# Thirteen weight loads sent as partitions 0 to 125 and 126 to 127

## What is computed

```
q = (x @ w_q).reshape(B, S, 8, 2, 128)
s = einsum('bshcd,cnd->bshcn', q, sub_keys)      # 8 heads, two sets of 128 keys
sv, si = top_k(s, 16)                            # best 16 of each set
best_s, pos = top_k(sums of all 16 x 16 pairs, 16)
gate = softmax(best_s)
hid = gelu(einsum('td,ted->te', xt, u[e]))       # 128 experts for each token
y   = einsum('te,ted->td', gate * hid, v[e])
```

## Time and profile before

| | |
|---|---|
| median of three runs | 1507.61 us |
| the profiled execution | 1510.85 us |
| its span, first to last instruction | 1508.9 us |
| TensorE, VectorE, ScalarE, GpSimd busy | 1340.3, 1015.8, 705.3, 492.7 us |
| moved by DMA | 597.94 MB, mean 396 GB/s |
| of it by gathers (q0) | 536.90 MB |
| of it by plain loads and stores (q1) | 60.01 MB |

### The profile page before, as it was taken

The page is one execution under the profiler, slowest core; times in us unless marked ns, Lnnn a source line. Parts: engine busy times, 40 slices in busy tenths (PEclk is TensorE's granted clock), DMA queues, the critical chain, the costliest instruction groups (busy, mean ns, idle before and its releaser), DMA issues.

```text
span 1508.9 us, 16214 instructions
## 1 busy us (share of the span) xinstructions
PE 1340.3 (89%) x5068; PEld 729.8 (48%) x5068; DVE 1015.8 (67%) x2399; ACT 705.3 (47%) x2128; POOL 492.7 (33%) x527
## 2 busy tenths in 40 slices
PE   9999998987898888889989899999989998888886
PEld 8877554433353454444447645444335443334322
DVE  1137877777757777686654587777787767666655
ACT  2223554545544545436554244654554544444443
POOL 0003333334333333333320233343333433333331
PEclk9999999999999999999999999999999999999999
DMA  9749999999999999999989699999999999999996
GB/s 370 252 168 412 384 419 420 420 421 422 421 421 421 421 421 421 421 420 405 421 348 410 238 405 420 421 421 422 421 422 421 416 422 421 422 421 420 412 423 265
DMA packets 92393, 597.94 MB, mean 396 GB/s; under 512 B 10386, under 2 KB 13074, under 8 KB 26004
## 3 DMA queue, kind: packets, MB, share of 16 engines
q0 software_dynamic: 73728, 536.90, 86.0%
q1 hardware_dynamic: 18580, 60.01, 10.5%
HBM read 595.82 MB, written 1.05 MB: 396 GB/s over the span
## 4 chain that ended last, share of the span: by engine, by line
PE 41%; DMA 29%; DVE 16%; ACT 9%; issue 3%; POOL 0%; SPq 0%; ACTq 0%; DVEq 0%; POOLq 0%
DMA uv<-in_peer_uv_dram,expert 28%; PE y L694 24%; DVE uv L1780 7%; PE spare L581 3%; PE y L540 3%; PE px L383 2%; ACT diag L1331 2%; PE y L408 2%; ACT L1323 2%; ACT wts L1325 1%; DVE key_idx L1628 1%; DVE hit L1620 1%; ACT act_hid L1323 1%; DVE key_idx L1622 1%; DVE key_top L1625 1%
## 5 line engine op out<-in xcount | busy, mean ns | idle before, releaser
L694 PE MATMUL y<-uv,diag 128*128 128x512 f32 x1868 | 911.7, 624 | 147.1 <-ACT diag L1331 146.2
L1780 DVE CUSTOM_DVE_ANT_0 uv<-px,uv 128x1024 f32<-128x1024 f32 x512 | 619.1, 1220 | 343.5 <-DMA uv<-in_peer_uv_dram,expert 334.3
L1158 POOL DMA_INDIRECT uv<-in_peer_uv_dram,expert x512 | 487.2, 952 | 961.4 <-PE y L694 752.5
L694 PEld LDWEIGHTS y<-uv,diag 128*128 128x128 f32 x1868 | 338.1, 195 | 581.8 <-issue 295.6
L1323 ACT ACTIVATE act_hid<-hid 128x1 f32<-128x1 f32 x512 | 102.8, 201 | 567.2 <-DVE hid L1780 563.1
L1331 ACT ACTIVATE diag<-ident,wts 128x128 f32<-128x128 f32 x468 | 187.9, 402 | 44.2 <-ACT wts L1325 1.5
L1325 ACT ACTIVATE wts<-act_hid,gate 128x1 f32<-128x1 f32 x512 | 150.7, 294 | 16.6
L1323 ACT ACT_TABLE_LOAD x47 | 60.3, 1283 | 0.8
L1791 DVE SCALAR_TENSOR_TENSOR vsum<-uv,wts,vsum 128x1024 f32<-128x1024 f32 x41 | 52.5, 1281 | 8.3 <-ACT wts L1325 8.0
L1780 DVE DVE_READ_ACCUMULATOR2_ANT hid<- 128x1 f32 x512 | 42.3, 83 | 0.0
L1497 DVE TENSOR_TENSOR probs<-spare,bias 128x320 f32<-128x320 f32 x16 | 7.6, 473 | 45.9 <-PE spare L436 45.9
(11 more groups left out here) (309 smaller groups left out, 1290.9 us busy)
## 6 DMA issues: line engine op xcount, KB each, us to landing
uv<-in_peer_uv_dram,expert POOLq DMA_INDIRECT x512, 13.6
uv<-in_na_w_dram SPq DMA_DIRECT2D x9, 512.0 KB, 8.9
w_q<-in_peer_w_q_dram SPq DMA_DIRECT2D x8, 512.0 KB, 11.8
uv<-in_mla_w_out_dram SPq DMA_DIRECT2D x8, 512.0 KB, 6.7
bias<-in_na_bias_dram SPq DMA_DIRECT2D x16, 160.0 KB, 7.0
w_vu<-in_na_w_dram SPq DMA_DIRECT2D x4, 512.0 KB, 9.0
w_latq<-in_na_w_out_dram SPq DMA_DIRECT2D x4, 512.0 KB, 6.7
latkv_room<-in_peer_w_q_dram SPq DMA_DIRECT2D x4, 512.0 KB, 11.0
```

Source lines behind the costliest of these rows:

```text
L694: last = T.matmul(Y[t][:, c, :], diag[:, acc_no(n) % DIAGS, :], uv[:, n % RING, 1, c * 512:(c + 1) * 512], start=False, stop=half_done)
L1158: pool.indirect_dma_start(uv[:, n % RING, :, :].rearrange("p h d -> p (h d)"), None, uv_table, bass.IndirectOffsetOnAxis(ap=expert[:, g % ...
L1780: V_.tensor_tensor_reduce(out=rows, in0=px[:, :, :], in1=rows, scale=1.0, scalar=0.0, op0=ALU.mult, op1=ALU.add, accum_out=hid[:, k:k + 1] ...
```

## The change

Thirteen loads of layer 0 are issued as two DMAs each, one for partitions 0 to 125 and one for 126 and 127. Source, target and order stay as they were. Each part adds 16 to the same semaphore, so the waits for them rise.

```
+LATE_KEPT = [4, 6, 7]
+SPLIT = 126
...
-                pe.wait_ge(s_kept[g % PH], 32 * (layer + 1))
+                pe.wait_ge(s_kept[g % PH], 32 * (layer + 1 + (g % PH in LATE_KEPT)))
...
-                    pe.wait_ge(s_latkv, 16)
+                    pe.wait_ge(s_latkv, 32)
...
-                    pe.wait_ge(s_latq, 16)
+                    pe.wait_ge(s_latq, 32)
...
-                pe.wait_ge(s_kn, 16)
+                pe.wait_ge(s_kn, 32)
...
-                pe.wait_ge(s_vu, 16)
+                pe.wait_ge(s_vu, 32)
...
-                    pe.wait_ge(s_qn, 16)
+                    pe.wait_ge(s_qn, 32)
...
-                    pe.wait_ge(s_qrs, 32)
+                    pe.wait_ge(s_qrs, 64)
...
+            def load_in_two(dst, src, done):
+                for part in (slice(0, SPLIT), slice(SPLIT, P)):
+                    sp.dma_start(dst[part], src[part]).then_inc(done, 16)
+
             def kept_load(layer, h):
                 for c in range(2):
+                    if layer == 0 and h in LATE_KEPT:
+                        load_in_two(kept[h][c], peer_w_q[layer, h, c], s_kept[h])
+                        continue
                     sp.dma_start(kept[h][c], peer_w_q[layer, h, c]).then_inc(s_kept[h], 16)
...
                         for dst, piece, done in loads[h]:
-                            sp.dma_start(dst, piece).then_inc(done, 16)
+                            load_in_two(dst, piece, done)
```

More of the change, by code:

```diff
@@ L1053, in layer_loads @@
                         sp.wait_ge(s_full[rest_bank(LATE[j])], job["rest", LATE[j]])
-                        kept_load(0, (4, 6, 7)[j])
+                        kept_load(0, LATE_KEPT[j])
                 if layer:
```

## The result

The changed kernel takes 1537.76 us (median of six runs, 1535.9 to 1541.02), against 1507.88 us for the kernel before on the same chip. The ratio is 1.0199, 95% interval 1.0185 to 1.0212: 29.9 us slower. The forecast was slower by 21 us, 1528.6; the time lies in its range.

The account below looks back on a forecast made before the run. The prediction took the last DMA engine in layer 0 as the bound; +26.9 us for rows meeting, less 6 us for the fetch-laden engine, gave +21 on 1507.6, so 1528.6 us; own range 1515 to 1542, overall range 1504 to 1542.

Parts of the forecast that it names:

- What bounds the kernel: Layer 0: gathers fill the DMA engines, dots start 2.48 us apart, and the last engine's work sets the layer's end.
- Issue and waits, priced 0: SP sends 13 more DMAs, 5 us in all but covered; TensorE waits have 41 us or more margin; both cost 0.
- Rows on the engines: Layer 0's cut loads: rows meet gather rows of the same partitions over another engine; +2.95 us per MiB, +26.9 us.
- an argument about turns: While a load comes in, each engine alternates gather and load rows, so is on its own partitions half the time.
- The 6 us taken off: End of layer 0: the last engine, slowed by instruction fetches, was 6 us behind; the new last one is not it.
- rival 3: No meeting of rows, but an engine with fetches has 9 or 10 rows: 1510.4 or 1513.3 us; chance 0.10.
- 1: Rival: engines alone, no meeting, spared engines have the fetches, an engine with 10 rows is last: 1506.5 us; chance 0.25.
- 2: Rival: no meeting, spared engines have the fetches, engines with 10 rows lead, other twelve set the pace: 1503.5; chance 0.14.
- 4: Rival: 126 rows still spread over 16 engines, 8 and 7, so nothing moves: 1507.6 us; chance 0.06.
- GB/s below 419 and fewer than 74 gathers: Sign in 420 to 620 us if rows meet, four gathers fewer; 421 GB/s and 74 gathers issued if not.
- 792.33 to about 813: Sign: issue of the second copy of the query weights moves from 792.33 to about 813; what follows keeps 716.6 us.
- The steps of some 0.93: Sign: extra delays between dots, 0.93 us the largest read, should become rare if engines with fetches are spared.

Follow-up runs that it names:

- the stages of DMAs alone: Separate kernel of DMAs alone, ten stages, gathers and loads of 1 MiB, whole or cut by partitions; beside gathers, whole loads took 72.3 us, the slowest cut 105.4.
- 112 + 16: Stage of the DMA-only kernel with 20 gathers beside 8 loads, each cut into 112 and 16 partitions, against whole loads: 90.7 us against 72.3.
- 126 + 2: Stage of the DMA-only kernel with 8 loads cut into 126 and 2 partitions, no gathers: 246 GB/s; the like stage beside gathers took 99.2 us, whole loads 72.3.

## Why the prediction was right, and where it was not

**What bounds the kernel: right.** The rate in the stretches and the dots moved together, and the 27.6 to 28.7 us by which layer 0 ends later in the profiled executions stand beside 29.9 us between the medians (25.1 between the two profiled spans).

**Issue and waits, priced 0: right,** by the halves of columns, 1.0007.

**Rows on the engines: right in kind and in size.** The term was +26.9 us, from half the rows meeting at 2.95 us for each MiB. The shift of layer 0 is 27.6 us, 3.02 for each. The half itself was a choice between 0.31 and 5.6, made by an argument about turns that was not measured, and that it came so near is partly luck: other cuts cost 2.3 to 4.1 us for each MiB in the stages of DMAs alone, so the share of rows that meet differs from cut to cut, and no run measured it. The mechanism, that the way into 8 partitions carries one engine's rate, is shown by the rates at 64, 32 and 16 partitions, and by 112 + 16.

**The 6 us taken off: wrong, and this is the step that leaves 1528.6 short of 1537.8.** It assumed that the last engine was 6 us behind the average one at the end of layer 0, and that the change makes up for this. By the landing records of the last gather of layer 0, the last of its sixteen parts lands 4.3 us after the mean of all in the kernel before, and 3.3 us after it in the changed kernel (2.7 in the five gathers ahead of it). So the last engine gained 1.0 us on the average one, 1.6 at most, and not 6. The mean itself moves by 29.7 us, the last part by 28.7. With nothing taken off, the sum would have been 1534.5.

The same records show why. The trace holds the landing time of each of the sixteen parts of a gather, though not which engine a part is. Here are, for some gathers of the changed kernel between 298 and 338 us, the first three and the last three parts, in us against a fixed clock of one gather each 2.483 us:

```
gather    1st    2nd    3rd  ...  14th   15th   16th
  66     -5.65  -4.98  -2.15     -0.46  -0.28   0.50
  68     -5.64  -4.98  -2.17     -0.29   0.08   0.44
  71     -5.66  -5.00  -2.17     -0.29   0.10   1.09
  75     -5.21  -5.01  -2.17     -0.30   0.10   1.09
  79     -2.54  -2.50  -2.20     -0.35   0.08   1.07
```

Two parts come 2.8 us and more ahead of all others; by all signs these are the two engines that the loads at 160 to 230 us spared, since with the cut at 112, which spares none, gather 64 has no such pair (its first three parts land within 0.15 us of each other). By gather 79 they have no work left to be ahead with. The last part takes a step of 0.65 at gather 71, and another part one of 0.96 (from -0.88) at gather 68. Steps of about these two sizes come back on two parts every 65 to 82 us in layer 1 of the kernel before, which is how often one of every two q14 fetches of the earlier trace rows comes; in the changed kernel q14 fetches start at 306.3 and 314.8 us, and gathers 68 and 71 land at 309 and 317. The q8 fetches step harder than the 0.93 that the forecast took for the largest: one starts at 302.9 and takes 1.03 us, and at gather 67 a part falls back by 1.5 us. These steps fall on other parts than the two leaders. So by these records the engines with the fetches are among the fourteen, the spared ones were not last here, and the best that the change could have brought by engines alone was rival 3, +2.8 to +5.7 us. Which numbers these engines have was not tried. Whether the remaining 2 us between 27.6 and 29.9 belong to anything but the spread of single executions is open.

**Rivals.** 1 and 2 needed engines alone; the rates by partitions and the cut at 112 rule that out. 3 has the same premise. 4 (126 rows still spread over 16 engines) falls by the share of 0.84 and the fourteen landing records. No run isolates the uneven rows; the 4 us between the cuts at 112 and at 126 may hold some of them.

**The signs that were named.** GB/s below 419 and fewer than 74 gathers: 387 and 68. Landing later than 15.2: 17.2. 792.33 to about 813: 819.89. The rest unchanged at 716.6: 714.1. Six gathers lost in 200 us, not four: five loads fall there, at some 3 us each, 15 us. The steps of some 0.93 were to become rare if the engines with the fetches were spared; they go on (0.96 at gather 68).

No run points to a version faster than the kernel before: whole loads were the fastest form in every comparison.

## What to carry to other kernels

Where gathers or loads already fill the DMA engines, judge a load by which engine carries the rows of which partitions, not by how many rows each engine has: 128 partitions in one DMA cost 2.49 us for each MiB beside gathers, and every cut by partitions tried here cost 2 to 4 us more. If a load must be cut, cut its columns. A DMA share of 1 says that the engines are taken, not that they move what they can; read it beside the GB/s.

## What the runs showed of the hardware

Beyond what the forecast leaned on: loads of 64 partitions alone run at 198 GB/s and of 16 at 106, with the engines at a share of 0.98 and 1.00, so that a queue of such loads looks saturated at a half or a quarter of the rate. Two halves of 64, sent one after the other, reach 220 GB/s together, not 416. The load of 126 alone does well (352 GB/s at 0.84), and 126 + 2 does badly (246 GB/s at 0.78, over a stretch that includes the slow end of its stage). It may be that two more rows on two engines, in loads that follow each other, are enough to put the engines out of step; that is not shown, since the first stage had eight loads in flight and the second four.
